# Block 2's gate and up tiles as seven half-size block products in place of eight, with one weight sum on GpSimd

## What is computed

```python
def rmsnorm(x, g):
    return x * lax.rsqrt(jnp.mean(x * x, axis=-1, keepdims=True) + EPS) * g

def swiglu(h, w_gate, w_up, w_down):
    return (jax.nn.silu(h @ w_gate) * (h @ w_up)) @ w_down

for l in range(2):
    x = x + 0.5 * swiglu(rmsnorm(x, ffn1_norm[l]), ffn1_w_gate[l], ffn1_w_up[l], ffn1_w_down[l])
    h = rmsnorm(x, mix_norm[l])
    ...                       # three kinds of attention
    x = x + o @ w_out[l]
    x = x + 0.5 * swiglu(rmsnorm(x, ffn2_norm[l]), ffn2_w_gate[l], ffn2_w_up[l], ffn2_w_down[l])
```

## Time and profile before

| | us |
|---|---|
| median of three runs | 3443.49 |
| the runs | 3441.7 to 3444.42 |
| span of the profiled execution | 3442.4 |

### The profile page before, as it was taken

How to read it: one execution, slowest core, us unless ns; L and a number is a source line. 1 busy time by engine, 2 the same in 40 slices (tenths; PEclk the granted TensorE clock), 3 DMA queues, 4 the chain that set the end, 5 groups by cost and what they waited for, 6 DMA issues and landing times. The chain is left out here.

```text
span 3442.4 us, 42159 instructions
## 1 busy us (share of the span) xinstructions
PE 3355.2 (97%) x15712; PEld 2626.8 (76%) x15716; DVE 1669.0 (48%) x2158; ACT 1222.1 (36%) x1831; POOL 238.6 (7%) x268
## 2 busy tenths in 40 slices
PE   8999999999999999999999999999999999999998
PEld 6667888775688877888775688887888776678887
DVE  6755443666444344443636554435443544654433
ACT  4343122432522233332444443324233344543233
POOL 1200000011000000000103300002000101300000
PEclk9999999999999999999999999999999989999999
DMA  6213322221243232332220133333332321023332
GB/s 169 63 48 86 97 98 97 86 80 49 73 103 95 98 104 73 97 98 98 75 64 25 38 103 97 97 98 94 96 94 97 86 74 32 20 86 98 97 98 67
DMA packets 434263, 288.19 MB, mean 84 GB/s; under 512 B 44529, under 2 KB 412317, under 8 KB 433897
## 3 DMA queue, kind: packets, MB, share of 16 engines
q1 hardware_dynamic: 431272, 280.02, 28.1%
q0 software_dynamic: 2736, 4.58, 0.9%
q10 hardware_dynamic: 144, 2.10, 0.2%
HBM read 284.53 MB, written 2.13 MB: 83 GB/s over the span
## 5 line engine op out<-in xcount | busy, mean ns | idle before, releaser
L2022 PE MATMUL bank<-hh,whi 128*128 128x512 f32 x2768 | 1093.3, 395 | 16.2 <-DVE hl L1470 7.2
L2023 PE MATMUL bank<-hl,whi 128*128 128x512 f32 x2768 | 1080.1, 390 | 0.0
L2024 PE MATMUL bank<-hh,wlo 128*128 128x512 f32 x2768 | 1079.9, 390 | 0.0
L1404 DVE TENSOR_TENSOR wlo<-raw,whi 128x1024 fp32r<-128x1024 f32 (+2 forms) x534 | 646.4, 1212 | 312.4 <-ACT whi L945 298.0
L945 ACT ACTIVATE whi<-raw 128x1024 fp32r<-128x1024 f32 (+2 forms) x534 | 546.4, 1034 | 258.3 <-PE bank L2024 257.9
L2022 PEld LDWEIGHTS bank<-hh,whi 128*128 128x128 f32 x2768 | 521.4, 188 | 150.3 <-issue 33.0
L2024 PEld LDWEIGHTS bank<-hh,wlo 128*128 128x128 f32 x2768 | 521.1, 188 | 109.4
L2023 PEld LDWEIGHTS bank<-hl,whi 128*128 128x128 f32 x2768 | 521.2, 188 | 108.3 <-issue 2.6
L2022 PE MATMUL bank<-fshi,whi 128*128 128x512 f32 (+1 forms) x1358 | 526.3, 388 | 3.6 <-ACT G L1090 1.6
L2023 PE MATMUL bank<-fslo,whi 128*128 128x512 f32 (+1 forms) x1358 | 522.6, 385 | 0.0
L2024 PE MATMUL bank<-fshi,wlo 128*128 128x512 f32 (+1 forms) x1358 | 522.5, 385 | 0.0
(11 more groups left out here) (257 smaller groups left out, 2565.9 us busy)
## 6 DMA issues: line engine op xcount, KB each, us to landing
raw<-in_ffn_w_gate SPq DMA_DIRECT2D x88, 512.0 KB, 3.8
raw<-in_ffn_w_up SPq DMA_DIRECT2D x88, 512.0 KB, 3.8
raw<-in_ffn_w_down SPq DMA_DIRECT2D x88, 512.0 KB, 3.5
raw<-in_w_in SPq DMA_DIRECT2D x78, 512.0 KB, 3.9
raw<-in_w_up SPq DMA_DIRECT2D x64, 512.0 KB, 4.0
raw<-in_w_down SPq DMA_DIRECT2D x64, 512.0 KB, 3.4
raw<-in_w_out SPq DMA_DIRECT2D x16, 512.0 KB, 4.0
raw<-in_w_in SPq DMA_DIRECT2D x18, 256.0 KB, 3.4
```

The lines of the kernel that those rows point to most:

```text
L1404: dve.tensor_tensor(slot3(wlo, s, m), slot3(raw, s, m), slot3(whi, s, m).bitcast(F32), ALU.subtract).then_inc(c.lo_done.sem, 1)
L2022: pe.matmul(o, wh, ah, start=start, stop=False)
L2023: pe.matmul(o, wh, al, start=False, stop=False)
L2024: return pe.matmul(o, wl, ah, start=False, stop=stop)
```

## The change

In each of the four ffns the first two pairs of gate and up (4 units) are made as before, and all of down. The other 40 units become 10 iterations. An iteration takes two tiles of gate and the same two of up, and sees the product of weights (two tiles of hidden features x 1024 rows) and activations (1024 rows x 512 tokens) as one of 2 x 2 blocks by 2 x 2 blocks: two feature tiles, two halves of the rows (512), two halves of the tokens (256). Instead of eight block products it makes seven (Winograd's form of Strassen's way), each, for up and for gate, 4 row tiles x 3 matmuls on 256 tokens: 24 matmuls a product (`few_product`), 168 an iteration.

- Sums of weights: four in an iteration. VectorE makes S3, S1 and S2 in place (`side_add`), GpSimd the fourth (`fourth_sums`), each of 128 x 1024 words. Every product's weights are then split by ScalarE (`side_high`) and VectorE (`side_low`).
- Sums of tokens: four in an ffn (`token_add`: TN1, TN2, T4, T3, on VectorE, from the gained x that ScalarE, four tiles, and GpSimd, four tiles, first write to `G`); they are split by `token_high` (ScalarE) and `token_low` (VectorE).
- Putting the products together: some are added in PSUM; ScalarE copies the first, second and third product of an iteration out (`copy_1`, `copy_5`, `copy_2`) and the last one with its sign turned (`negated`); VectorE makes three combinations (`combine`). TensorE's third product goes on adding to the bank of the first and so waits for `copy_1`. `gate_scaled`, the silu and `f_product` follow one iteration later, on 1024 elements each. Up is not scaled by `rstd` there any more; in `down` VectorE scales the f tiles from the third on instead.
- Loads: the weights of an iteration, four DMAs of 512 KB (`quads`), go to all four slots of `raw` in odd iterations and to `tab` in even ones. The first set waits until all four slots are free; the table in `tab` is loaded again in each layer, by GpSimd behind its sums.
- Silu's table is loaded once in an ffn. The loops over the units of gate and up become written-out code.

The diff, cut to its core:

```diff
...
+S3, S1, S2 = 1, 2, 3
+TN1, TN2, T3, T4 = 1, 2, 3, 4
...
+            def quads(c, l, which):
+                up, gate = (("ffn1_w_up_2", "ffn1_w_gate_2"), ("ffn2_w_up_2", "ffn2_w_gate_2"))[which]
+                for i in range(1, ITERS + 1):
+                    if i == 1:
+                        sp.wait_ge(c.lo_done.sem, c.lo_done.at(l, ffn0[which] + UPS))
+                    elif i == 2 and which:
+                        sp.wait_ge(c.x_ready.sem, c.x_ready.at(l, KT + 1))
+                    elif i == 2 and l:
+                        sp.wait_ge(c.s_lo.sem, c.s_lo.at(l - 1, 2 * VIRTUAL))
+                    elif i == 2:
+                        sp.wait_ge(c1.x_ready.sem, c1.x_ready.at(LAYERS - 1, KT))
+                    else:
+                        sp.wait_ge(c.s_lo.sem, c.s_lo.at(l, product(which, i - 2, FEW - 1)))
+                    for t in range(2):
+                        for h, name in enumerate((up, gate)):
+                            tile = (2 * i + t) * P
+                            dst = ring(i)[:, h, t, :].rearrange("p (k n) -> p k n", k=KT)
+                            src = w[name][bass.ds(l, 1), :, tile:tile + P].rearrange("a (k p) n -> p (a k) n", p=P)
+                            sp.dma_start(dst, src).then_inc(quad_in[i % 2][2 * h + t], 16)
+                sp.wait_ge(c.s_lo.sem, c.s_lo.at(l, product(which, ITERS - 1, FEW - 1)))
...
+            def gained(c, l, b0, gains):
+                pool.wait_ge(c.rn_lo.sem, c.rn_lo.at(l, b0 + KT))
+                for k in range(NK, KT):
+                    pool.tensor_scalar(G[:, B_TEMP + k * S:B_TEMP + k * S + S], x[:, k, :], gains[:, k:k + 1], None, ALU.mult).then_inc(c.b_pool.sem, 1)
+            def fourth_sums(c, l, which):
+                for i in range(1, ITERS + 1):
+                    a1, b0 = ring(i)[:, :, 0, 512:1024], ring(i)[:, :, 1, 0:512]
+                    pool.wait_ge(c.s_lo.sem, c.s_lo.at(l, product(which, i, 3)))
+                    pool.wait_ge(c.s_add.sem, c.s_add.at(l, added(which, i, S2)))
+                    pool.tensor_tensor(a1, a1, b0, ALU.add).then_inc(c.s_add4.sem, 1)
...
+                gained(c, l, 0, prm[:, P2_F1:P2_F1 + KT])
+                fourth_sums(c, l, 0)
+                pool.wait_ge(c.s_lo.sem, c.s_lo.at(l, VIRTUAL))
+                pool.dma_start(tab[:, 0:2048], tab2).then_inc(tab_in, 16)
...
+            def side_high(c, l, which, i, p):
+                n = FEW * (i - 1) + p
+                s = product_slot(l, which, n)
+                if p == 0:
+                    turn = (2 * l + which) * (ITERS // 2) + (i + 1) // 2
+                    for landed_ in quad_in[i % 2]:
+                        act.wait_ge(landed_, 16 * turn)
+                if i == 1 and p < RING:
+                    act.wait_ge(c.group_done.sem, c.group_done.at(l, b2["last_of"][ffn0[which] + p]))
+                else:
+                    act.wait_ge(c.s_prod.sem, c.s_prod.at(l, VIRTUAL * which + n - RING + 1))
+                if p in (1, 2, 4):
+                    act.wait_ge(c.s_add.sem, c.s_add.at(l, added(which, i, {1: S1, 2: S2, 4: S3}[p])))
+                elif p == 5:
+                    act.wait_ge(c.s_add4.sem, c.s_add4.at(l, ITERS * which + i))
+                act.activation(paired(whi, s), side(i, p), ACT.Copy).then_inc(c.s_hi.sem, 1)
+            def token_high(c, l, which, t):
+                act.wait_ge(c.t_add.sem, c.t_add.at(l, 4 * which + {TN1: 1, TN2: 2, T4: 3, T3: 4}[t]))
+                if t == T3:
+                    act.wait_ge(c.group_done.sem, c.group_done.at(l, b2["last_of"][ffn0[which] + UPS - 1]))
+                act.activation(t_split(t, 0), t_temp(t), ACT.Copy).then_inc(c.t_hi.sem, 1)
+            def copy_1(c, l, which, i):
+                act.wait_ge(c.s_prod.sem, c.s_prod.at(l, product(which, i, 0)))
+                if i > 1:
+                    act.wait_ge(c.s_cmb.sem, c.s_cmb.at(l, combined(which, i - 1, CB_11)))
+                act.activation(tmp[0], bank[:, i % 2, :], ACT.Copy).then_inc(c.s_cp.sem, 1)
...
+            def mlp(l, which, gains):
+                n0 = ffn0[which]
+                def first_silu(t):
+                    act.wait_ge(c.g_norm.sem, c.g_norm.at(l, 2 * which + t + 1))
+                    act.activation(rt[t], tmp[t], ACT.Silu).then_inc(c.silu.sem, 1)
+                act.preload_act_table_set(SILU_SET)
+                for k in range(NK):
+                    act.activation(G[:, B_TEMP + k * S:B_TEMP + k * S + S], x[:, k, :], ACT.Copy, scale=gains[:, k:k + 1]).then_inc(c.b_act.sem, 1)
+                side_high(c, l, which, 1, 0)
+                first_silu(0)
+                token_high(c, l, which, TN1)
+                side_high(c, l, which, 1, 1)
+                side_high(c, l, which, 1, 2)
+                first_silu(1)
+                token_high(c, l, which, TN2)
+                side_high(c, l, which, 1, 3)
+                token_high(c, l, which, T3)
+                token_high(c, l, which, T4)
+                copy_1(c, l, which, 1)
+                side_high(c, l, which, 1, 4)
+                copy_5(c, l, which, 1)
+                side_high(c, l, which, 1, 5)
+                copy_2(c, l, which, 1)
+                side_high(c, l, which, 1, 6)
+                for i in range(2, ITERS + 1):
+                    side_high(c, l, which, i, 0)
+                    side_high(c, l, which, i, 1)
+                    negated(c, l, which, i - 1)
+                    side_high(c, l, which, i, 2)
+                    side_high(c, l, which, i, 3)
+                    copy_1(c, l, which, i)
+                    side_high(c, l, which, i, 4)
+                    gate_silu(c, l, which, i - 1)
+                    copy_5(c, l, which, i)
+                    side_high(c, l, which, i, 5)
+                    copy_2(c, l, which, i)
+                    side_high(c, l, which, i, 6)
+                down(c, b, l, n0 + UPS, T2 * which, T2, c.f2_done, which)
             for l in range(LAYERS):
...
+                    if scaled and t + LOOK < nt:
+                        f = f_tile(t + LOOK + (0 if i is None else i * 4))
+                        dve.tensor_tensor(f, f, rstd, ALU.mult).then_inc(c.f2_done.sem, 1)
...
+            def side_low(l, which, i, p):
+                n = FEW * (i - 1) + p
+                s = product_slot(l, which, n)
+                dve.wait_ge(c.s_hi.sem, c.s_hi.at(l, VIRTUAL * which + n + 1))
+                dve.tensor_tensor(paired(wlo, s), side(i, p), paired(whi, s).bitcast(F32), ALU.subtract).then_inc(c.s_lo.sem, 1)
+            def side_add(l, which, i, s):
+                u = ring(i)
+                a0 = u[:, :, 0, 0:512]
+                b0, b1_ = u[:, :, 1, 0:512], u[:, :, 1, 512:1024]
+                to, one, two = {S3: (a0, a0, b0), S1: (b0, b0, b1_), S2: (b0, a0, b1_)}[s]
+                if s != S1:
+                    dve.wait_ge(c.s_lo.sem, c.s_lo.at(l, product(which, i, {S3: 0, S2: 1}[s])))
+                if s != S3:
+                    dve.wait_ge(c.s_add.sem, c.s_add.at(l, added(which, i, s) - 1))
+                dve.tensor_tensor(to, one, two, ALU.add).then_inc(c.s_add.sem, 1)
+            def token_add(l, which, t):
+                done = c.t_add
+                if t == TN1:
...
+            def combine(l, which, i, s):
...
+            def gate_scaled(l, which, i):
...
+            def f_product(l, which, i):
+                dve.wait_ge(c.s_silu.sem, c.s_silu.at(l, ITERS * which + i))
+                f, gate = (G[:, F_AT + 1024 * j:F_AT + 1024 * (j + 1)] for j in (i, i + 1))
+                dve.tensor_tensor(f, f, gate, ALU.mult).then_inc(c.s_f.sem, 1)
+            def mlp(l, which, r):
+                n0, q0 = ffn0[which], 2 * which
...
+                first_gate(0)
+                first_up(0)
+                side_low(l, which, 1, 0)
+                token_add(l, which, TN1)
+                side_add(l, which, 1, S3)
+                side_add(l, which, 1, S1)
+                first_f(0)
+                token_low(l, which, TN1)
+                side_low(l, which, 1, 1)
+                side_add(l, which, 1, S2)
+                token_add(l, which, TN2)
+                first_gate(1)
+                side_low(l, which, 1, 2)
+                token_low(l, which, TN2)
+                first_up(1)
+                first_f(1)
+                side_low(l, which, 1, 3)
+                token_add(l, which, T4)
+                token_add(l, which, T3)
+                token_low(l, which, T3)
+                token_low(l, which, T4)
+                for p in range(4, FEW):
+                    side_low(l, which, 1, p)
+                for i in range(2, ITERS + 1):
+                    combine(l, which, i - 1, CB_11)
+                    side_low(l, which, i, 0)
+                    side_add(l, which, i, S3)
+                    combine(l, which, i - 1, CB_22)
+                    side_add(l, which, i, S1)
+                    combine(l, which, i - 1, CB_12)
```

(55 more changed lines are left out.)

## The result

The changed kernel takes 3452.46 us (median of 8 runs, 3450.96 to 3454.33), the one before 3443.91 us in the same comparison: a ratio of 1.0026, 95% interval 1.0016 to 1.0035. It is slower, by a little more than a measurement can tell from no change. The profiled execution has a span of 3449.2 us, 6.8 more than before. It was the fastest of the eight (3450.96 us; each run's time lies some 1.8 us above its own span).

A forecast was written before the change was run, and what follows sets the result against it. TensorE's matmul stream was taken to bound the kernel: 3442.4 - 64.0 (products) + 65.0 (starts) + 8 (clock) = 3451.4 us of span, plus 1.1 to the median, 3452.5 us; range 3425 to 3505.

The forecast's parts named there:

- the likeliest case: Whole kernel: products save, starts and clock take it back; 3452.5 us, held within 3443 to 3465; chance 0.48.
- The products: Gate and up iterations: 256-column matmuls at 0.120 us, laps of 20.16 against 21.76 us; -64.0 us over four ffns.
- The faster rival: Products' matmuls of 256 columns cost only 0.1116 us, so VectorE's 19.7 us sets the lap; 3435 us, chance 0.22.
- The starts: Each ffn's third product waits for `copy_1` behind VectorE's first sums and low parts; 14.2 to 17.3 us each, +65.0 us.
- the late landing: Start of ffn2, both layers: first weight DMAs land at +9.2, 3.1 us after ScalarE is ready, making 17.3 us.
- the chain: Start of each ffn: VectorE's 13 operations of 1.23 and four of 0.69 up to T3, 18.8 us before waits.
- The clock: Behind the idle at each ffn's start the granted clock falls; 2.0 us per start taken, +8 us in all.
- the slower rival: In the iterations VectorE's lap reaches about 21.2 us, over TensorE's 20.16; +40 us, 3490 us, chance 0.25.
- the hand-offs of the rival: In each iteration, waits between ScalarE and VectorE of some 0.1 us at each of a dozen places lengthen VectorE's lap.
- The turn to `down`: Where products end and `down` begins: no stall, as first casts of down's weights run beside the last products.

The follow-up runs named there:

- e3: Changed kernel with eight units per ffn made the old way, nine iterations, token sums laid beside units 3 to 8: 3385.50 us, ratio 0.9835 to the kernel before.
- e1: Changed kernel with ScalarE copying the first product out before casting T3 and T4: 3438.02 us, ratio 0.9984 to the kernel before.
- e2: Changed kernel with VectorE making the fourth weight sum in place of GpSimd: 3445.88 us, ratio 1.0016 to the kernel before.
- e4: Changed kernel with GpSimd making its weight sum twice in each iteration: 3523.76 us in a single run, beside 3445.95 before.

## Why the prediction was right

The forecast was 3452.5 us, the median 3452.46, in the likeliest case's own range; the direction and the case are the ones forecast. That the numbers meet so closely is partly luck. I took 4.6 us too many for the starts and left out 2.1 elsewhere, so the span was 3449.2, not 3451.4. The median lies 3.3 us above that span, not the 1.1 that I took, because the profiled execution was the fastest of its eight, and this makes up the difference. Term by term:

**The products.** 0.120 us for a matmul of 256 columns is what the rows show, and the lap of 20.16 holds to the hundredth in e3. -64.0 us is right. The faster rival fell with it: 256 columns are not as cheap as the 0.1116 of 64. The Trainium skill (TensorE: Matmul & The Clock Gate, Back-to-back issue gap) has 109 ns for a lone matmul of this size; the trace has 120 in this stream, and the measurement decides.

**The starts.** The mechanism was right in the main: four waits for `copy_1`, none in the later iterations, with VectorE's work behind them (e1, and e3, where it has room). The waits themselves are 10.7 to 12.2 us, not the 14 to 17 that were foreseen. How late the third product is, with the wait before the second product and the slow clock behind that wait, is 12.8 (18.52 - 5.76), 15.8, 15.9 and 15.9 us, together 60.4; forecast were 14.2, 17.3, 16.2 and 17.3, together 65.0. The first ffn shows where the difference comes from. Its unit 2 and ScalarE's four gained copies:

```profile
1308.08 0.80 PE L2369 MATMUL bank<-hb,whi 128*128 128x512 f32 x1
1311.35 2.56 ACT L1496 ACTIVATE G<-x,prm 128x512 f32<-128x512 f32 x4
```

Four small things make up the 1.4 us. The first product begins 11.3 us behind unit 2, not 10.9, so the third would be due 0.5 later. The four gained copies take 2.56 us, not 2.9, and the first cast ends at +6.8, not +7.2. VectorE needs 20.4 us from its first low part (1314.90) to the end of T3, not 20.7. I took its 17 operations at the durations of the earlier trace rows, but back to back they follow each other closer than they last: T4 at 1330.77 lasts 1.22 and T3 begins at 1331.91, 1.14 later, and 17 x 0.09 is 1.5 us, less where one waits for the one ahead. Against it stands that T3 was held 2.1 us by GpSimd (3.36 for 1.23), not the 1.4 that I took. From T3's end to the third product it is 2.7 us, not 2.9. The second product of this ffn does not wait, as I had thought it would. In ffn2 the late landing was sized well. Its rows are the first load, the first cast and the second product:

```profile
2008.73 0.37 SPq L926 DMA_DIRECT2D raw<-in_ffn_w_up  x1
...
2018.10 1.06 ACT L1314 ACTIVATE whi<-raw 128x1024 fp32r<-128x1024 f32 x1 [2.94 <-DMA raw<-in_ffn_w_gate]
...
2026.88 0.55 PE L2869 MATMUL bank<-fb,whi 128*128 128x256 f32 x1 [3.19 <-DVE wlo L2130]
```

The cast waits 2.94 us for the last of the four DMAs, 9.4 us behind the first's issue (9.8 forecast), and the second product comes 3.19 late. In ffn1 of layer 1 the size was met by luck (15.9 for 16.2). The loads did not land in time, as I had them:

```profile
2370.66 0.37 SPq L926 DMA_DIRECT2D raw<-in_ffn_w_up  x1
...
2381.34 1.06 ACT L1314 ACTIVATE whi<-raw 128x1024 fp32r<-128x1024 f32 x1 [1.17 <-DMA raw<-in_ffn_w_gate]
```

The first cast waits 1.17 us and begins 10.7 behind the first issue. VectorE's operations beside GpSimd's gained tiles lose the rest, some 1.8 us where I took 2: the wait that I missed and the chain that I took too long nearly cancel.

**The clock.** 8 us were taken with nothing in the trace to go by but one dip of 1.6 and no idle of that length, so that it came out is luck. What is left of the 68.7 us lost is 68.7 - 60.4 = 8.3, from 1.4 to 2.4 a start. In the windows behind a wait (TensorE: busy, granted clock, DMA share, GB/s):

```profile
1338.00:1341.00 3.00, 3.00 (x15) 0.52 0.03 5
2027.00:2030.00 3.00, 3.00 (x14) 0.50 0.00 0
2042.00:2047.00 5.00, 4.76 (x22) 0.50 0.01 3
```

15 matmuls in 3 us instead of 25: 0.20 each, at about half of the full clock (the lower level). In ffn2 it falls twice, behind the second product's wait and behind the third's; the first fall lies inside the later wait and costs nothing.

**The rest.** -64.0 + 60.4 + 8.3 = +4.7; the span has 6.8. The 2.1 left lie outside the four stages, where I had put nothing. By the distances between the four units 2, before and after, 0.8 us are lost ahead of the first ffn and 3.4 between the two ffns of layer 0, and 2.2 are won between those of layer 1. One place is seen in windows of TensorE, behind the same wait of 2.05 us in the attention of layer 0, before and after:

```profile
1719.20:1722.20 3.00, 2.96 (x14) 1.00 0.38 112
1719.80:1722.80 3.00, 3.00 (x8) 0.50 0.44 122
```

In layer 1 it is the other way round: the clock behind that wait is 0.51 before (2783.4) and 1.00 after (2788.6). No run settles what moves these stretches. In e3, with no wait at the starts, 1.0 us is left so.

**VectorE as the bound** (the slower rival). Its price was right at the upper end: a low part beside GpSimd's sum takes 3.23 us in the iterations,

```profile
1459.15 3.23 DVE L2130 TENSOR_TENSOR wlo<-raw,whi 128x1024 fp32r<-128x1024 f32 x1 [0.33 <-ACT whi L1314]
```

2.0 more, where I took 1.5. It still did not set the lap: VectorE is busy 90.43 of 100 us, 18.2 a lap where I had 18.3, and TensorE does not wait. That operations back to back cost less than counted is one reason. Why the hand-offs of the rival, some 1.2 us, do not lengthen the lap was not tested. That VectorE's own sum would cost about the same as GpSimd's was close, and erred to GpSimd's favour (e2: 86.08). The Trainium skill (GPSIMD Engine Reference, 8. Key points) says that GpSimd shares its way to the memory with VectorE and that operations with two inputs there contend. The trace agrees, with 3.25 for 1.23, and shows how: the two take turns.

**The turn to `down`** has no wait, as forecast.

## What to carry to other kernels

A faster inner loop has to be paid for where it starts: count the work that the first iteration needs, engine by engine, against the work that TensorE still has at that point, and put in as much of the old way as covers it. Here one iteration less in each ffn (6.4 us in all), with the sums laid out beside the units that took its place, turned 8.5 us lost into 57 us won. And before a sum is given to GpSimd to spare VectorE, look at a VectorE row that runs beside GpSimd: here the help cost more than the work.

## What the hardware showed that was not expected

- GpSimd and VectorE take turns on operations with two operands in memory: 3.25 us for a low part of 1.23 beside a sum of 2.42, and 3.27 for a sum begun beside a low part.
- VectorE's operations of 128 x 1024 that do not need each other's results follow each other every 1.14 us though each lasts 1.22.
- Matmuls of 256 columns come every 0.120 us: the 13 ns above columns/2.4 GHz are about the same as at 512 columns and, by the mean of 0.174 of the eight pairs, at 384.
- The same wait of 2.05 us before the same matmuls had the full clock behind it in one execution and 0.50 in the other (1719.2 before, 1719.8 after). In e4 a wait of 2.20 us at 1412.07 had 0.50 behind it and one of 2.20 at 1456.86 the full clock. How long the engine idles does not alone decide it.
